# Token rows finished on ScalarE by way of a root-weighted diagonal, and the first expert's rows picked already turned

## What is computed

```
h2   = rms_norm(x, norm2_w) * (1 + sc2) + sh2        # sc2, sh2: per sequence
comb = route(h2, w_router, router_bias)              # 16 experts, 2 for each token
out  = sum over e of comb[:, e] * ((silu(h2 @ wg[e]) * (h2 @ wu[e])) @ wd[e])
x    = x + g2 * out                                  # then a last rms_norm
```

## Time and profile before

| | |
|---|---|
| time, median of 3 runs | 1017.1 us (1016.8 to 1017.32) |
| the profiled execution | 1015.97 us, of which the span 1014.2 us |
| TensorE busy | 980.0 us, 97% of the span |
| VectorE, ScalarE, GpSimd busy | 443.5, 236.0, 139.9 us |
| mean granted TensorE clock | 0.988 |

### The profile page before, as it was taken

How to read it: one execution, slowest core, us unless ns; L and a number is a source line. 1 busy time by engine, 2 the same in 40 slices (tenths; PEclk the granted TensorE clock), 3 DMA queues, 4 the chain that set the end, 5 groups by cost and what they waited for, 6 DMA issues and landing times.

```text
span 1014.2 us, 20467 instructions
## 1 busy us (share of the span) xinstructions
PE 980.0 (97%) x8514; PEld 742.1 (73%) x8514; DVE 443.5 (44%) x1084; ACT 236.0 (23%) x469; POOL 139.9 (14%) x230
## 2 busy tenths in 40 slices
PE   5999999999999999999999999999899999999996
PEld 2667667667766666666666767667699999999981
DVE  3121234676346986656651530123443324334226
ACT  2240122233263322242252300002231101011013
POOL 0000132353021353432310000000200000000020
PEclk8999999999999999999999999999899999999998
DMA  9863344564455556655443533342468999999993
GB/s 379 323 219 107 142 166 128 190 225 164 163 194 192 227 193 209 221 206 211 157 172 124 222 121 125 124 166 96 185 274 309 421 421 423 423 422 424 421 374 110
DMA packets 47157, 237.64 MB, mean 234 GB/s; under 512 B 6800, under 2 KB 11248, under 8 KB 23792
## 3 DMA queue, kind: packets, MB, share of 16 engines
q1 hardware_dynamic: 45120, 230.85, 59.6%
q0 software_dynamic: 1520, 5.34, 1.6%
q10 hardware_dynamic: 448, 0.50, 0.2%
HBM read 212.31 MB, written 24.36 MB: 233 GB/s over the span
## 4 chain that ended last, share of the span: by engine, by line
PE 91%; DVE 4%; ACT 2%; issue 1%; DMA 1%; POOL 0%; DVEq 0%; SPq 0%; POOLq 0%; ACTq 0%
PE pjB L833 16%; PE pjA L833 15%; PE states L1394 11%; PE pjA L1218 7%; PE pjB L1218 7%; PE states L1397 6%; PE pjA L1394 2%; PE pjB L1394 2%; PE states L842 2%; PE pjB L1397 1%; PE pjA L1397 1%; PE bank L1182 1%; PE bank L957 1%; PE states L1197 1%; PE states L957 1%
## 5 line engine op out<-in xcount | busy, mean ns | idle before, releaser
L833 PE MATMUL pjB<-hF,ring 128*128 128x320 f32 x608 | 173.5, 439 | 0.0
L833 PE MATMUL pjA<-hF,ring 128*128 128x320 f32 x608 | 171.9, 436 | 0.5 <-ACT regA L1641 0.5
L1394 PE MATMUL states<-ring,oF 128*32 128x128 f32 x1488 | 165.1, 273 | 0.8 <-ACT G L1849 0.8
L1397 PE MATMUL states<-ring,oF 128*32 128x384 f32 x1488 | 165.3, 491 | 0.0
L1394 PEld LDWEIGHTS states<-ring,oF 128*32 128x32 f32 x1488 | 162.3, 110 | 1.1 <-ACT G L1849 1.0
L833 PEld LDWEIGHTS pjB<-hF,ring 128*128 128x128 f32 x608 | 114.2, 192 | 49.3 <-issue 5.9
L833 PEld LDWEIGHTS pjA<-hF,ring 128*128 128x128 f32 x608 | 113.2, 190 | 50.6 <-issue 7.0
L2657 DVE TENSOR_TENSOR oF<-oF,states 128x384 f32<-128x384 f32 x15 | 8.3, 554 | 145.4 <-PE states L1397 145.4
L2687 DVE STREAM_TRANSPOSE hF<-oF 32x96 f32<-32x96 f32 x240 | 64.8, 270 | 4.6
L2383 DVE TENSOR_TENSOR G<-G 128x320 f32<-128x320 f32 x32 | 48.8, 1562 | 0.0
L1995 POOL TENSOR_TENSOR G<-regA,G 128x128 f32<-128x128 f32 (+1 forms) x32 | 19.0, 593 | 196.3 <-ACT G L1697 196.3
(11 more groups left out here) (523 smaller groups left out, 1409.3 us busy)
## 6 DMA issues: line engine op xcount, KB each, us to landing
ring<-in_w SPq DMA_DIRECT2D x171, 1024.0 KB, 8.3
G<-in_ss SPq DMA_DIRECT2D x16, 512.0 KB, 3.9
out_ss_new<-G SPq DMA_DIRECT2D x16, 512.0 KB, 2.8
G<-csd SPq DMA_DIRECT2D x16, 320.0 KB, 3.5
G<-in_sg SPq DMA_DIRECT2D x4, 1024.0 KB, 6.4
out_sg_new<-G SPq DMA_DIRECT2D x16, 256.0 KB, 2.8
yd<-hF SPq DMA_DIRECT2D x14, 288.0 KB, 7.0
rF<-in_w SPq DMA_DIRECT2D x2, 1024.0 KB, 9.9
```

The costliest lines, as they stand in the source:

```text
L833: mm = pe.matmul(pj[g % 2][:, 0:T], w[:, k, half * P:half * P + P], hF[:, k, :], start=(k == 0), stop=(k == KT - 1))
L1394: pe.matmul(bank[CAP:P, c * P:(c + 1) * P], rows(c, True), w[:, WIDE:512], start=first and c == 0, stop=last, tile_position=(0, CAP), skip ...
L1397: mm = pe.matmul(bank[QUAD * c:QUAD * c + QUAD, 0:WIDE], rows(c, False), w[:, 0:WIDE], start=first, stop=last, tile_position=(0, QUAD * c) ...
```

## The change

- **Row turns.** `shift_rows` is gone. GpSimd builds `diag`, a 128 by 1024 row of eight diagonal blocks with the prompt's shift on the diagonals, once the merge is done, and multiplies the sample tokens' shifts `shX` by `rst` once that is there. `turn_u(n)` now first puts `root x shift` into the bank (for t < 2 by one product of `rst` with 512 columns of `diag`, for t = 2 by four products of `shX` with the identity), and adds the turned `hF` by four ordinary matmuls with the identity in place of transposes. ScalarE copies the bank to `hT` with the scale `r3`, so the root cancels at the shift; VectorE's six instructions are gone, and ScalarE's six copies of shifts with them.
- **Order on TensorE.** `turn_u(0)` moves behind the logits, all six turns follow each other, then `turn_late(0)` and `turn_late(1)`, and only then `ranks`; then `turn_late` 2, 4, 5, 3.
- **Rows of expert 0.** For each of 8 feature tiles and 3 token tiles one product with 128 features of `hT` stationary and the 96 columns of `selE` moving: the result comes out feature-major. `rowsE`, its copies and transposes are gone; ScalarE copies the first half to `heF`, VectorE the second, and that one is waited for only ahead of the second half of expert 0's gate product.
- **Order on VectorE.** `selE` directly after `idx`, then `meta`.
- The DMA of line 779 waits for `s_oss` to reach GH + 2 (all picks done).

The core of the diff (left out: the renumbered constants, ScalarE's list `LATE` of copies, the waits' new counts):

```diff
@@ turn_u
+                bank = turn_bank[n]
+                if t < 2:
+                    pe.matmul(bank[:, :], rst[:, c0:c1], diag[:, half * 512:half * 512 + 512], start=True, stop=False,
+                              skip_group_check=True)
                 for k in range(4):
-                    mm = pe.transpose(turn_bank[n][0:rows, k * P:k * P + P], hF[:, 4 * half + k, c0:c1], ident)
-                mm.then_inc(s_ht, 1)
+                    f = 4 * half + k
+                    if t == 2:
+                        pe.matmul(bank[0:rows, k * P:k * P + P], shX[:, f, :], ident, start=True, stop=False,
+                                  skip_group_check=True)
+                    mm = pe.matmul(bank[0:rows, k * P:k * P + P], hF[:, f, c0:c1], ident, start=False, stop=True,
+                                   skip_group_check=True)
                 mm.then_inc(s_ht, 1)
@@ TensorE's order
-            turn_u(0)
             pe.wait_ge(s_nsd, 2)
...
-            shift_rows()
+            pe.wait_ge(s_osd, 2)
+            turn_u(0)
             pe.wait_ge(s_rst, 4)
-            turn_u(1)
-            for n, copied in ((2, 2), (3, 3), (4, 5), (5, 7)):
-                pe.wait_ge(s_rta, copied)
+            for n in range(1, 4):
                 turn_u(n)
+            pe.wait_ge(s_osd, 3)
+            for n in range(4, 6):
+                turn_u(n)
...
-            for n in range(3):
+            for n in (0, 1):
                 turn_late(n)
+            (ranks, as before, now here)
+            for n in (2, 4, 5, 3):
+                turn_late(n)
             pe.wait_ge(s_dsp, DISPATCH_FIRST)
-            for t, (c0, c1, rows) in enumerate(TT):
-                pe.wait_ge(s_htc, 2 * t + 2)
-                for h in range(2):
-                    mm = pe.matmul((b[3], b[0])[h][0:CAP, :], selE[0:rows, t, :], hT[0:rows, t, 512 * h:512 * h + 512],
-                                   start=(t == 0), stop=(t == 2))
-            mm.then_inc(s_oss, 1)
-            turn_late(3)
-            turn_late(4)
-            pe.wait_ge(s_rqc, 4)
+            pe.wait_ge(s_htc, 6)
             for k in range(KT):
-                mm = pe.transpose(pj[k // 4][:, k % 4 * CAP:(k % 4 + 1) * CAP], rowsE[:, k * P:k * P + P], ident[0:CAP, 0:CAP])
-            mm.then_inc(s_oss, 1)
-            turn_late(5)
+                for t, (c0, c1, rows) in enumerate(TT):
+                    mm = pe.matmul((b[3], b[0])[k // 4][:, k % 4 * CAP:(k % 4 + 1) * CAP], hT[0:rows, t, k * P:(k + 1) * P],
+                                   selE[0:rows, t, :], start=(t == 0), stop=(t == 2))
+                if k % 4 == 3:
+                    mm.then_inc(s_oss, 1)
@@ ScalarE
-            for t, half in ((2, 0), (2, 1), (0, 0), (1, 0), (0, 1), (1, 1)):
+            act.wait_ge(s_rst, 4)
+            for n, (t, half) in enumerate(TURNS):
                 rows = TT[t][2]
-                act.wait_ge(s_ht, 3 if t < 2 else 2)
-                act.activation(hT[...], (pj if t == 2 else b[4:6])[half][0:rows, :], ACT.Copy).then_inc(s_rta, 1)
+                act.wait_ge(s_ht, n + 1)
+                act.activation(hT[...], (b[3], b[0], pj[0], pj[1], b[4], b[5])[n][0:rows, :],
+                               ACT.Copy, scale=r3[0:rows, t:t + 1]).then_inc(s_htc, 1)
@@ GpSimd
+            pool.wait_ge(s_mxv, 24)
+            pool.wait_ge(s_mod, 17)
+            pool.tensor_tensor(diag.rearrange("p (k c) -> p k c", k=KT), ident.unsqueeze(1).to_broadcast([P, KT, P]),
+                               mod[:, 24:32, 0:1].to_broadcast([P, KT, P]), ALU.mult).then_inc(s_osd, 1)
+            pool.wait_ge(s_nsd, 2)
+            pool.tensor_tensor(shX, shX, rst[:, NP_:T].unsqueeze(1).to_broadcast([P, KT, NSAMP]), ALU.mult).then_inc(s_osd, 1)
@@ VectorE
-            for n, (t, half) in enumerate(TURNS):
-                ...
-                dve.scalar_tensor_tensor(y_, (b[3], b[0], pj[0], pj[1], b[4], b[5])[n][0:rows, :], r3[0:rows, t:t + 1], y_,
-                                         ALU.mult, ALU.add).then_inc(s_htc, 1)
```

More of the change, by code:

```diff
@@ L130 @@
 DISPATCH_IDX = 7
-DISPATCH_META = 10
-DISPATCH_FIRST = DISPATCH_META + 4
-DISPATCH_STEPS = DISPATCH_FIRST + 8
+DISPATCH_FIRST = DISPATCH_IDX + 4
+DISPATCH_META = DISPATCH_FIRST + 3
+DISPATCH_STEPS = DISPATCH_META + 8
 TM_EARLY = 6
@@ L1337, in turn_late @@
                     pe.wait_ge(s_htc, 6)
-                elif n:
+                elif n == 0:
+                    pe.wait_ge(s_rtv, ROUTER_LOGITS)
+                else:
                     pe.wait_ge(s_tmc, n if n < 4 else n - 1)
@@ L1352, in turn_late @@
                 mm.then_inc(s_tm, 1)
-            for n in range(3):
+            for n in (0, 1):
+                turn_late(n)
+            pe.wait_ge(s_rtv, ROUTER_OS)
+            ranks = b[1][:, 64:64 + 4 * E]
+            flat_os = os_.rearrange("p a b -> p (a b)")
+            pe.matmul(ranks, upper, flat_os, start=True, stop=True)
+            for t in range(1, 4):
+                mm = pe.matmul(ranks[:, t * E:], ones, flat_os[:, 0:(4 - t) * E], start=False, stop=True,
+                               skip_group_check=True)
+            mm.then_inc(s_rank, 1)
+            for n in (2, 4, 5, 3):
                 turn_late(n)
             pe.wait_ge(s_dsp, DISPATCH_FIRST)
-            for t, (c0, c1, rows) in enumerate(TT):
-                pe.wait_ge(s_htc, 2 * t + 2)
-                for h in range(2):
-                    mm = pe.matmul((b[3], b[0])[h][0:CAP, :], selE[0:rows, t, :], hT[0:rows, t, 512 * h:512 * h + 512],
-                                   start=(t == 0), stop=(t == 2))
-            mm.then_inc(s_oss, 1)
-            turn_late(3)
-            turn_late(4)
-            pe.wait_ge(s_rqc, 4)
-            for k in range(KT):
-                mm = pe.transpose(pj[k // 4][:, k % 4 * CAP:(k % 4 + 1) * CAP], rowsE[:, k * P:k * P + P], ident[0:CAP, 0:CAP])
-            mm.then_inc(s_oss, 1)
-            turn_late(5)
+            pe.wait_ge(s_htc, 6)
+            for k in range(KT):
+                for t, (c0, c1, rows) in enumerate(TT):
[3 more added lines that the diff above has]
+                    mm.then_inc(s_oss, 1)
             def turn_tokens(t):
@@ L1408, in gate_up @@
                         w = moe_chunk(pe, e, 2 * part + half)
+                        if isinstance(e, int) and e == 0 and half and not part:
+                            pe.wait_ge(s_rqc, 3)
                         for k in range(4):
@@ L1464, in _ @@
             with pe.If(few(pe)):
[L1465 to L1466 removed]
+                pe.wait_ge(s_tmc, 6)
+                pe.wait_ge(s_ysd, 2)
                 def one(e, v):
@@ L1849, in copy_late @@
                 act.activation(dst[0:rows, half * 512:half * 512 + 512], tm_bank[n][0:rows, :], ACT.Copy).then_inc(s_tmc, 1)
-            for n in range(3):
+            for n in LATE[:6]:
                 copy_late(n)
             act.wait_ge(s_oss, GH + 1)
[L1854 to L1859, removed]
+            act.activation(heF[:, 0, 0:4, :], b[3][:, 0:4 * CAP].rearrange("p (k c) -> p k c", c=CAP), ACT.Copy).then_inc(s_ysd, 1)
             def squared(n, t, rows, src):
@@ L2588, in _ @@
             assert ds_.n == DISPATCH_FIRST, ds_.n
-            dve.wait_ge(s_rta, 7)
-            for n, (t, half) in enumerate(TURNS):
-                rows = TT[t][2]
-                dve.wait_ge(s_ht, 3 + n if n else 1)
-                y_ = hT[0:rows, t, half * 512:half * 512 + 512]
-                dve.scalar_tensor_tensor(y_, (b[3], b[0], pj[0], pj[1], b[4], b[5])[n][0:rows, :], r3[0:rows, t:t + 1], y_,
-                                         ALU.mult, ALU.add).then_inc(s_htc, 1)
+            dstep(dve.tensor_scalar(mf[:, 0:E], mf[:, 0:E], 1.0, None, ALU.add))
+            dstep(dve.tensor_reduce(mf[:, E:E + 1], cnt, AX.X, ALU.max))
+            dstep(dve.tensor_copy(meta[:, :], mf))
+            assert ds_.n == DISPATCH_META, ds_.n
             dstep(dve.tensor_tensor(pos[:, 1].rearrange("p (a b) -> p a b", a=3), ranks,
```

36 lines of the change are left out of this document (7 added, 29 removed).

## The result

| | median of the runs | runs | median of before beside it | ratio to before, 95% interval |
|---|---|---|---|---|
| changed kernel | 1018.6 us (1016.42 to 1024.23) | 20 | 1016.93 us, 20 runs | 1.0026 [1.0017, 1.0036] |
| once more (e9) | 1018.82 | 8 | 1017.2 | 1.0026 [1.0006, 1.0046] |
| once more (e12) | 1018.2 | 8 | 1017.22 | 1.0018 [0.9998, 1.0038] |
| once more (e13) | 1018.72 | 8 | 1017.22 | 1.0040 [1.0014, 1.0065] |

The account below looks back on a forecast made before the run. It took TensorE, busy 97% of the span, as the bound, with the path moving to its turns; longer turns and later ranks against cheaper picks left 0.8 us gained: 1017.1 - 0.8 = 1016.3 us, range 1014.6 to 1019.5.

Parts of the forecast that it names:

- I take 0.11, the nearest in width: 5.3 us: Picks of expert 0's rows on TensorE: 48 records at 0.11 us each, 5.3 us together, ending at 725.6.
- the 6.5 that the prediction named as a sign of being wrong: Sign for the picks: the prediction is wrong if they take under 4.5 or over 6.5 us.
- Branch: I keep 0.9: Between the last pick and the expert loop's first matmul: 0.9 us as before, or 0.1 if quite hidden.
- the forecast of -0.8: Start of the expert loop: at 726.5 instead of 727.31, 0.8 us earlier, and the whole time shorter by as much.
- A slack of 3.0 us has shrunk to 0.2: Read-back of line 779 lands at 740.75; the third turn_tokens wants it at 740.9, so no cost but no further gain.
- this rival: Read-back binds at line 1379: each us of later landing is a us lost, 1 us gives 1017.3; chance 0.18.
- The clock rival: TensorE's waits near 715 and 719 halve its clock for late turn, ranks and picks: 1019.2 to 1020.3; chance 0.17.
- the stretch from 716 to 724 that was to decide: Test for the falling clock: it holds if a granted clock of 0.5 covers more than 2 us between 716 and 724.

Follow-up runs that it names:

- e9: The changed kernel, unedited, measured and profiled again: median 1018.82 us, ratio to before 1.0026; its profiled execution took 1023.12 us.
- e12: The changed kernel, unedited, measured a third time: median 1018.2 us, ratio to before 1.0018; its profiled execution took 1017.57 us.
- e13: The changed kernel, unedited, measured a fourth time: median 1018.72 us, ratio to before 1.0040; its profiled execution took 1017.81 us.
- e10: e5 with ranks multiplied right behind the fourth turn, late turns left in place: 1015.97 us, ratio to before 0.9996.
- e1: The changed kernel with pick products grouped by row count, 3 changes instead of 15 (expert 0's rows come out wrong): 1017.34 us, ratio to before 1.0013.
- e5: The changed kernel with the third token tile padded by zeros to 128 rows in the picks: 1018.98 us, ratio to before 1.0028.
- e11: e6 with the changed kernel's 64-row third token tile in the picks: 1017.13 us, ratio to before 1.0005.
- e6: e5 with ranks behind the fourth turn and five late turns put between the picks: 1013.89 us, ratio to before 0.9976.
- e3: The changed kernel with expert 0's rows picked the old way, selE stationary: 1019.83 us, ratio to before 1.0034.
- e7: The kernel before with only turn_u(0) moved behind the logits and selE put ahead of meta: 1015.77 us, ratio to before 0.9994.
- e4: The kernel before with only the new picks, hT stationary and selE moving, old turns kept: 1026.26 us, ratio to before 1.0103.

## Why the prediction was wrong

**The step that failed: "I take 0.11, the nearest in width: 5.3 us".** The size of a record was right, and what stands between records of unlike rows was missing: 8.03 us were measured, over the 6.5 that the prediction named as a sign of being wrong. Of 48 records 16 have 64 stationary rows; each of these 8 products lies alone between pairs of products with 128. Weight loads of e12, grouped by form (busy, mean ns, idle before):

```profile
L1365 PEld LDWEIGHTS states<-oF,regA 128*128 128x128 f32 x16 | 2.1, 190 | 1.4 <-DVE oF L2586 1.1
L1365 PEld LDWEIGHTS bank<-oF,regA 128*128 128x128 f32 x16 | 2.1, 190 | 0.4
L1365 PEld LDWEIGHTS states<-oF,regA 64*128 64x128 f32 x8 | 1.2, 184 | 0.4
L1365 PEld LDWEIGHTS bank<-oF,regA 64*128 64x128 f32 x8 | 1.2, 184 | 0.4
```

The same in e10, where all have 128 rows:

```profile
L1365 PEld LDWEIGHTS bank<-oF,regA 128*128 128x128 f32 x24 | 2.8, 192 | 0.0
L1365 PEld LDWEIGHTS states<-oF,regA 128*128 128x128 f32 x24 | 2.8, 192 | 0.0
```

A load lasts as long in both, about 190 ns. With equal rows each begins while the one before it still runs, 24 in 2.8 us, and the load engine is never idle. With alternating rows the overlap breaks off at each change: 6.6 us busy and about 0.4 idle in each of the four groups, against 5.6 and 0.0. By the timelines the picks are 8.03 us against 5.42, so 2.61 over 16 changes (15 among the picks, one into the loop): 0.16 us each. The first half alone, where nothing else changes, gives 4.01 against 2.65, or 0.17 for each of 8 changes. e1 with three changes among the picks in 6.02 us, e5 with none in 5.52 and e11 against e6 (+2.24) agree; in e1 eight records of 64 rows in a row took no longer each than those of 128, so it is the change that costs and not the shape. The 5.3 us were right for the kernel that I priced (5.42 and 5.52), not for this one.

The trace of before had this price. In the chain of waits, at full clock, these rows stand beside those of the earlier trace rows:

```profile
722.49 1.02 PE states L1360 x2
...
724.37 0.59 PE states L1346 x4
724.96 0.44 PE bank L1346 x4
```

The third pair of old picks goes from 128 to 64 rows: 1.02 us for its first product against 0.86 for its second, so 0.16 for the change. The late turn behind them goes back to 128: 0.59 against 0.44, though here the kind of product changes as well. The prediction itself uses two prices for a group of four turns, 0.59 at 702.75 and 0.43 elsewhere, and doesn't ask where the difference comes from. Which changes cost was not tested further. The group of 702.75 has as many rows as the product ahead of it but other stationary columns (128 behind 32), and so have the sample turns (64 behind 128 at 711.95 in e12, 0.27 us to the next start where 0.22 is the pace), while the late turns of before go from 128 to 64 columns at no price (724.96).

The Trainium skill (TensorE: Matmul & The Clock Gate, Part 3: Packing small matmuls — row/col tiling, The mechanism) says that a weight load overlaps with running matmuls only when it goes to another row group; the same section also has loads into a background weight buffer pulled ahead. This case's traces don't bear the "only" out: in e10 all loads go to the same 128 rows and overlap with the matmuls (24 of each in 2.8 us), and a change of the rows is where the overlap ends.

**"Branch: I keep 0.9"** was wrong in the other direction, by 0.9. The timeline of before has more in the row at 727.31 than the chain of the earlier trace rows:

```profile
727.31 0.49 PE L1394 MATMUL states<-ring,oF 128*32 128x128 f32 x3 [0.77 <-ACT G L1849]
```

The profile puts that idle time down to a copy, not to the load of `meta`. In e3 and e7, with the same end, 0.33 us are put down to VectorE's copy of the turned half. The changed kernel has neither copy at its end, and the load of `meta` in e12 (667 ns, start 726.2) runs beside the picks:

```profile
L535 PEldq TENSOR_LOAD <-meta x1: 667/667/667, 726.2 to 726.2; - x1
```

The loop's first matmul follows the last pick with no gap. How much of the old 0.9 was copy and how much branch was not separated. The two sizes together: +2.7 in the picks, -0.9 in the branch and +0.3 ahead of the picks make +2.1 on the forecast of -0.8, so +1.3, and the profiles show +1.26. The errors of the two terms have opposite signs, so that the second hid a third of the first; that 1018.6 lies within the stated range of 1014.6 to 1019.5 is luck in this sense, and also because the upper part of the range was there for the clock, which the usual runs don't need.

**"A slack of 3.0 us has shrunk to 0.2"** misread the code. The read-back of `hT` raises the same semaphore as that of the second half of `xs01`, and the second `turn_tokens` waits for both, not the third. It began 12.65 us behind the loop start before (739.96), and the data had landed at 738.74: slack 1.2. In e12 it begins at 741.86 and the data land 8.9 us behind the issue,

```profile
732.02 1.96 SPq L780 DMA_DIRECT2D regA<-xd  x1
```

at 740.9: 0.9 us of slack, so nothing was lost to it in the changed kernel as it is. But had the picks cost 5.3, the loop would have started at 726.5, the rows been wanted at 739.2 and landed at 740.3 (as in e1 and e12) to 741.7 (as in e5), all in the time of before. e1 (0.96 us) and e5 (2.8 us) show just this wait. So the forecast gain of 0.8 would have gone to the read-back even if the picks had cost 5.3; this rival held 0.18 in the prediction and was the next limit behind the picks.

**The clock rival** held 0.17. A fall came in two profiles of four and, by their times and mean clocks, in 10 of 44 runs. But it was not the one described: it began at 724.8 (723.7 in the time of before), not at 716, with TensorE busy without a break since 721.57, so that hardly 0.3 us of it lie in the stretch from 716 to 724 that was to decide. It cost more than 2.9 to 4.0: the stage 29.45 - 25.78 = 3.7, and 5.1 us of the loop at half speed (733.27 to 738.4) some 2.5 more. It sets the spread of the changed kernel, not its median. What decides between the kinds in one and the same program is open.

**Right.** The path moved to TensorE's turns and the first late turns; the whole schedule up to the picks held within 0.3 us. ScalarE's copies fitted under the turns (0.69 us each, here in the dear execution):

```profile
708.96 0.69 ACT L1840 ACTIVATE regA<-bank,G 128x512 f32<-128x512 f32 x1 [1.00 <-PE bank L1282]
```

and GpSimd's product with `shX` took 1.26 us (1.1 expected) and held nobody up.

**Left open.** 0.4 us between the medians beyond the 1.26 of the stage; and how often before, whose profiled stage had the clock at half from 713.5 for 6.8 us, goes without that fall. A profile of before at full clock was not taken. Of the 102 runs of before beside the experiments 26 have a mean clock of 0.991 or 0.992, against 0.988 in the profiled one, and took 1014.75 to 1015.74; the other 76 took 1016.05 to 1018.39. If those 26 are the ones without the fall, which no profile shows, the loss against them is larger.

## What to carry to other kernels

Price a run of short products by its order as well as by its shapes: products with unlike numbers of stationary rows belong in groups, or are padded to one number, since zeros cost nothing here and each change 0.16 to 0.17 us. Before counting a gain, find the transfer that the next stage waits for and compute its slack from the semaphore that the waiting instruction names; a late chain of small steps (ranks, indices, scatters) is worth moving ahead of bulk work that nobody waits for. Where the runs are of two kinds, one profile shows only one of them.

## What was new of the hardware

- TensorE: 48 float32 records with 96 moving columns took 5.42 us with 128 stationary rows in all, 8.03 us with every third product at 64 rows, and 6.02 us with the same products grouped by rows.
- The granted clock fell to 0.5 in the middle of picks that kept TensorE busy in every window around it (0.50 of 0.50 us), for 13.65 us, in two of four profiles of the same program; e4's lasted 23.9 us.
